# Prompt attention of a hybrid decoder step: a head's weight piece issued behind the AV products instead of right behind the scores

## The reference

```
q, k, v, qi, ki, wi, gq, gk, gv, og, a1, gt = split(h @ w_in)       # one input projection
# branch A: sparse attention; an indexer picks 256 causal keys per query
sc  = where(causal, sum_h wi * relu(qi . ki), -inf);  idx = top_k(sc, 256)
s   = where(valid, q . k[idx] * 64**-0.5, -inf)
att = softmax(s) @ v[idx]                                          # 16 heads, 4 KV heads, head width 64
# branch B: gated linear attention in chunks of 64; gla = rmsnorm(o) * silu(og)
merged = sigmoid(gt0) * (att @ w_proj_attn) + sigmoid(gt1) * (gla @ w_proj_gla)
h = LN(alpha*h + merged @ w_out);  h = LN(alpha*h + relu(h @ w_up)**2 @ w_down)
```

## Time and profile before

| | |
|---|---|
| median of three runs | 3179.45 us (3174.3 to 3191.85) |
| the profiled execution, its own time | 3178.85 us |
| its span in the trace | 3176.9 us |
| mean granted clock of TensorE | 0.924 |
| TensorE matmul busy | 2779.1 us, 87% of the span |
| VectorE, ScalarE, GpSimd busy | 1488.3, 654.4, 569.1 us |
| prompt attention | from about 731 to 1364.8 us |

### The profile page before, as it was taken

How to read it: one execution, slowest core, us unless ns; L and a number is a source line. 1 busy time by engine, 2 the same in 40 slices (tenths; PEclk the granted TensorE clock), 3 DMA queues, 4 the chain that set the end, 5 groups by cost and what they waited for, 6 DMA issues and landing times.

```text
span 3176.9 us, 42244 instructions
## 1 busy us (share of the span) xinstructions
PE 2779.1 (87%) x15803; PEld 2407.3 (76%) x15803; DVE 1488.3 (47%) x2861; ACT 654.4 (21%) x1156; POOL 569.1 (18%) x264
## 2 busy tenths in 40 slices
PE   3968999948999999958889996879899999999996
PEld 3968889948888899845556654769887878788884
DVE  5057999982455545123333425421634343434336
ACT  2033211102233344111223323210310000001011
POOL 4201122210100000100000000122421222222223
PEclk9979999979999999978889968889899999999998
DMA  4142322213211111155434334241111111111001
GB/s 180 56 103 55 105 93 86 85 44 90 76 56 53 31 45 40 55 147 152 143 106 141 113 111 146 99 160 36 39 40 40 40 40 40 40 40 40 26 26 56
DMA packets 173658, 244.03 MB, mean 77 GB/s; under 512 B 49889, under 2 KB 147330, under 8 KB 164146
## 3 DMA queue, kind: packets, MB, share of 16 engines
q1 hardware_dynamic: 139890, 204.03, 20.0%
q10 hardware_dynamic: 33600, 37.80, 3.5%
HBM read 180.00 MB, written 59.08 MB: 75 GB/s over the span
## 4 chain that ended last, share of the span: by engine, by line
PE 65%; DVE 20%; issue 6%; ACT 3%; DMA 2%; SPq 2%; DVEq 2%; POOL 1%; ACTq 0%; POOLq 0%; PEldq 0%
PE ps L955 6%; DVE masks L1694 6%; PE ps L1218 4%; PE ps L1219 4%; PE ps L1220 4%; PE ps L1238 4%; PE ps L1240 3%; PE ps L1239 3%; PE ps L835 2%; DVE maskS L1694 2%; PE ps L836 2%; PE ps L837 2%; PE ps L1059 2%; PE ps L943 2%; PE ps L757 2%
## 5 line engine op out<-in xcount | busy, mean ns | idle before, releaser
L411 POOL TENSOR_TENSOR pool_go<-pool_go 128x1 f32<-128x1 f32 x73 | 15.1, 207 | 2498.0 <-PE ps L837 780.3
L414 POOL TENSOR_TENSOR w_lo<-raw,w_hi 128x2048 fp32r<-128x2048 f32 x73 | 352.8, 4833 | 10.9 <-issue 0.5
L1238 PE MATMUL ps<-w_hi,a_hi 128*128 128x512 f32 (+1 forms) x576 | 241.6, 419 | 66.9 <-DVE res L2080 60.2
L835 PE MATMUL ps<-xt_hi,w_hi 128*128 128x368 f32 x768 | 260.9, 340 | 0.7
L2080 DVE TENSOR_TENSOR res<-res,ps 128x512 f32<-128x512 f32 (+1 forms) x270 | 181.7, 683 | 169.3 <-PE ps L1240 169.3
L1218 PE MATMUL ps<-xt_hi,w_hi 128*128 128x368 f32 x768 | 254.3, 331 | 3.4 <-SPq L368 3.4
L836 PE MATMUL ps<-xt_lo,w_hi 128*128 128x368 f32 x768 | 257.3, 335 | 0.0
L837 PE MATMUL ps<-xt_hi,w_lo 128*128 128x368 f32 x768 | 256.4, 334 | 0.0
L1219 PE MATMUL ps<-xt_lo,w_hi 128*128 128x368 f32 x768 | 254.6, 332 | 0.0
L1220 PE MATMUL ps<-xt_hi,w_lo 128*128 128x368 f32 x768 | 254.1, 331 | 0.0
L1240 PE MATMUL ps<-w_lo,a_hi 128*128 128x512 f32 (+1 forms) x576 | 236.5, 411 | 0.0
(11 more groups left out here) (286 smaller groups left out, 6348.4 us busy)
## 6 DMA issues: line engine op xcount, KB each, us to landing
raw<-w_stream SPq DMA_DIRECT2D x73, 1024.0 KB, 5.0
kpg<-cache_k SPq DMA_DIRECT2D x128, 128.0 KB, 2.2
qT_d<-kT ACTq DMA_DIRECT2D x48, 184.0 KB, 1.9
gate_d<-kT ACTq DMA_DIRECT2D x48, 184.0 KB, 1.9
gst<-gate_d SPq DMA_DIRECT2D x16, 552.0 KB, 5.7
gvog_d<-kT ACTq DMA_DIRECT2D x64, 128.0 KB, 1.9
qraw<-qT_d SPq DMA_DIRECT2D x64, 128.0 KB, 3.1
vpg<-cache_v ACTq DMA_DIRECT2D x64, 128.0 KB, 2.5
```

Source lines behind the costliest of these rows:

```text
L414: pool.tensor_tensor(w_lo[:, s, :], raw[:, s, :], w_hi[:, s, :].bitcast(F32), ALU.subtract).then_inc(w_split, 1)
L835: pe.matmul(out, hi, xt_hi[:, k, cols], start=k == 0, stop=False)
L1238: pe.matmul(out, a_hi[:, a, k, cols], w_hi[:, s, w], start=k == 0, stop=False)
```

## The change

In the loop over head steps on TensorE the piece is issued last, behind the third transpose batch and the AV products of the previous head, instead of right behind the scores. Nothing else is edited.

```diff
@@ -969,13 +969,13 @@
                     tr(hh, j)
                 if hh + 2 < NH * NT:
                     qk(hh + 2)
-                if f < fills_by(hh):
-                    fill(f)
-                    f += 1
                 if nb == 3:
                     tr(hh, 2)
                 for j in range(batches_of((hh - 1) // NH) if hh else 0):
                     av(hh - 1, j)
+                if f < fills_by(hh):
+                    fill(f)
+                    f += 1
             av(NH * NT - 1, 0)
             barrier(pe, 3)
```

## The result

| | before | after |
|---|---|---|
| median of four runs, us | 3176.88 (3172.53 to 3191.85) | 3215.03 (3210.82 to 3236.06) |
| profiled execution, own time | 3178.85 | 3214.59 |
| its span | 3176.9 | 3212.8 |
| mean granted clock | 0.924 | 0.918 |

The ratio is 1.012, 95% interval 1.0079 to 1.0162: slower by 1.2%. The forecast was 3188, with 3176 to 3198 as its range. It had the sign right and the size wrong by a factor of four: the spans differ by 35.9 us where 9 were forecast.

What follows compares the result with a forecast made beforehand. TensorE was taken to bound the loop, waiting mainly for VectorE's query split. Terms 2.5 + 0.2 + 2.5 + 1.2 + 0.4 = 6.8 us, plus 2 for the clock, about 9, gave 3188 us; range 3176 to 3198.

Steps and rivals of the forecast that it cites:

- The swap, 0: Tiles 1 to 7, 28 pieces: swapping AV products and piece on TensorE keeps the sum, 0 us.
- Tile 0, +2.5: Tile 0, heads 1, 5, 9, 13: AV products leave the split's cover, four waits grow by 0.63 us, 2.5 us.
- Tile 8, +0.2: Tile 8: four AV blocks cost 1.0 us, a hidden wait at the end gives -0.81 us; sum +0.2 us.
- GpSimd, +2.5: Three query splits on VectorE collide longer with GpSimd's weight subtraction: +0.85, +1.1, +0.55, sum 2.5 us.
- Exp behind the copy, +1.2: Tile 1, heads 17 to 33: transposes wait for ScalarE's Exp behind its piece copy, 1.2 us.
- Tile 7's last head, +0.4: Third transpose batch, now right behind tile 8's tiny scores, waits for an evacuation, +0.4 us.
- The clock, +2: Longer waits make one or two more stretches at 1.2 GHz likely, 1.25 us lost each: +2 us, ends 0 and 14.
- the difference lies in 731 to 1365 us: The prompt attention loop: a difference outside this stretch would make the whole prediction wrong.
- 26 us is the most the loop could win: Score matmul L927's waits for query split L1766, 26.0 us in 32 times, cap the change's gain, 0.8% of the span.
- B: Rival: eleven grown or new waits each bring a stretch at 1.2 GHz, 14 plus 6.8 us, 3200 us; chance 0.12.
- A: Rival: nothing measurable, moved blocks absorbed because waits end on something that doesn't move with the piece; 3179 us; chance 0.20.
- C: Rival: faster, earlier AV products let VectorE's split go ahead, at most 14 us won, 3165 us; chance 0.04.

Runs made afterwards that it cites:

- e1_tile0: Changed order in tile 0 of the loop alone, otherwise the kernel before: 3177.24 us, loop 626.0 us.
- e3_tile8: Changed order in tile 8 of the loop alone, otherwise the kernel before: 3183.49 us, loop 631.9 us.
- e6_three_back: The kernel after with the pieces of head steps 23, 47 and 71 put back ahead of the AV products: 3217.25 us, loop 651.2 us.
- v1: The kernel before with pieces between transposes and scores in steps hh % 4 == 2, those of tiles 1 to 7 due one step earlier: 3140.44 us, ratio 0.9884.
- e5: The kernel after with ten extra transposes (1.1 us) ahead of the gated linear attention: 3237.51 us, ratio 1.0172.
- e8: The kernel after with 21 extra transposes ahead of gated linear attention head 0 and 26 ahead of each of heads 1 to 3: 3212.74 us, ratio 1.013.
- e2: Changed order in tiles 1 to 7 of the loop alone, otherwise the kernel before: 3210.81 us, loop 642.8 us.
- e11: The kernel after with ten extra transposes (1.1 us) ahead of the head loop: 3216.91 us, loop 649.4 us.
- e7_before_aligned: The kernel before with 26 extra transposes (2.8 us) ahead of each of gated linear attention heads 1, 2 and 3: 3160.29 us, ratio 0.9952.

## Why the prediction was wrong, point by point

1. **The swap, 0.** Nearly. Tiles 5 and 6, with neither half clock nor a changed wait to speak of, grew by 0.24 and 0.28 us with four pieces each: about 0.07 us per piece, 2 us over the 28. It lies inside the bounds of 0.1 us each way; which seam costs it I haven't separated.
2. **Tile 0, +2.5.** Right: 2.07 us per wait where 1.97 was worked out, 28.9 - 26.0 = 2.9 us in e1_tile0. The length didn't show it, since the clock gave as much back (8 us less at 1.2 GHz).
3. **Tile 8, +0.2.** The score waits grew by 1.2 us (e3_tile8; +1.0 was the term). The end went as forecast, with the AV products directly behind the last piece and no wait:

```profile
1379.09 0.33 PE L837 MATMUL ps<-xt_hi,w_lo 128*128 128x368 f32 x1
1379.35 0.35 PE L955 MATMUL ps<-vnat,kT 16*80 16x64 f32 x2
```

   Not foreseen: where the loop's steps are this short the next piece meets the copy of the last one, L835 for L1329, 0.7 us in three times.
4. **GpSimd, +2.5.** The sum was right to a tenth, its parts (0.85, 1.1, 0.55) to 0.16, in both directions; the 1.5 us of the third leaves out the 0.1 us of lead-in and would be 1.6. Timeline of after, tiles 1, 3 and 4:

```profile
844.15 4.50 POOL L414 TENSOR_TENSOR w_lo<-raw,w_hi 128x2048 fp32r<-128x2048 f32 x1
...
845.46 3.75 DVE L1766 TENSOR_TENSOR ql<-qraw,qh 128x512 fp32r<-128x512 f32 x1
...
928.52 2.39 DVE L1766 TENSOR_TENSOR ql<-qraw,qh 128x512 fp32r<-128x512 f32 x1
...
1027.56 1.34 DVE L1766 TENSOR_TENSOR ql<-qraw,qh 128x512 fp32r<-128x512 f32 x1
```

   Against 3.06, 1.23 and 0.68 us that is +0.69, +1.16 and +0.66, 2.5 us. The first ends at 849.21, 0.56 us behind L414's 848.65; the two collisions of before ended 0.56 and 0.54 us behind theirs (847.08 and 925.15); the other two of after end 0.54 us behind theirs (930.37 and 1028.36), though the three of after had started 3.2, 1.9 and 0.8 us ahead of that end. e6_three_back takes exactly these 2.5 us away again. The Trainium skill's page "SBUF — State Buffer" states under "Who interferes with whom" that the later of two such operations is locked out until the other is done, and the sum rested on it; these five collisions with one and the same distance of 0.54 to 0.56 us agree.
5. **Exp behind the copy, +1.2.** The waits at L943 for ScalarE rose by 0.6 us (1.1 after, 0.5 before), of which 0.2 lie at the loop's first transposes, ahead of any piece of it; three of 0.08 us in tile 1 are too short for that row. Half the term.
6. **Tile 7's last head, +0.4.** Right, 0.32 us:

```profile
1282.26 0.33 PE L943 MATMUL ps<-ident,pP 128*128 128x128 f32 x1 [0.32 <-DVE kT L1793]
```

   With these, part 1 and the copies, the direct costs come to 6.6 + 0.6 + 0.7 + 0.3 (less the 0.5 of the earlier trace rows that went, plus 2.0 of the swap), 9.7 us against the 6.8 forecast. Counted the other way, TensorE's idle time in the loop rose from 25.5 to 33.6 us, 8.0, and with the 2.0 of the swap that is 10.
7. **The clock, +2: the term that was mis-sized.** Measured were 18.1 - 9.7 = 8.4 us in the loop, for 19 us more at 1.2 GHz, 0.44 each; 18 starts against 29 had given 0.38. So the price was near, and the amount was not that of one or two stretches of 3.3 us but of about six. It came as two longer stretches in tiles 1 and 3 (10.2 and 13.7 us) rather than as many short ones. I had argued from tile 8's clock of 0.98 that waits of this kind mostly don't bring it on; that row held in one order of the work and not in the other.

**The step that failed altogether** was not in the list: that the difference lies in 731 to 1365 us. The text itself said that the whole would be wrong otherwise. The stages behind were taken to start later and else run as they were, and 22.4 of the 35.9 us came from the one scan that didn't. Without it the spans would differ by 13.5 us, and the time, about 3192, would lie in the range. It could have been priced. The trace of before holds four scans of the same instructions, one of which takes 49.7 us where three take 29.9; I passed over it, because the change doesn't touch that stage. What the runs showed in its place: the scan of head 0 takes 49.8 us after and 29.9 before, by where the granted clock stands when it starts. A range with such a slow scan in it would have reached to about 3188 + 22 = 3210, and with the clock's end of 14 us in the loop beyond 3215.

One more sentence of the prediction fell: that 26 us is the most the loop could win. v1 won 42.7 us there, since each wait costs more than its idle time and brings half clock with it.

**The rivals.** B had the mechanism and too low a price: half clock was 8 us in the loop as it worked out for six stretches, and another 20 us in a place that it didn't name. The Trainium skill's page "TensorE: Matmul & The Clock Gate", section "HAM oscillation — how this bites in real kernels", by which repeated waits bring the half clock back each time, tells of a case with waits of 3 to 5 us each. Here waits of 0.5 to 3.8 us brought it, some of them and not each time: it fits v1 (no wait in the loop, 5 us at 1.2 GHz) and not e1_tile0 (2.9 us more wait, 8 us less at 1.2 GHz). Its "Part 1: The HAM clock gate (the "warmup" mystery)" puts the loss of warming up at under 1% of a typical span and calls it variable from run to run, by the phase in which the kernel starts. Half clock here is not one such loss at the start: this one scan alone turned 0.7% of the span. A fell (waits moved by what was worked out), C fell (no wait shrank).

**What stays open.** Whether a given execution's scan falls to 1.2 GHz: the distance from the last fall sorts the scans afterwards, and nothing here told e5 or e8 ahead. Why the wait ahead of head 0 brings no fall in four of the six traces with late pieces in tiles 1 to 7 (after, e2, e5, e8), and its scan is slow, isn't shown either; e6_three_back, with a loop 7 us longer than after's, escaped. Why the new order has 48 to 72 us of it and the old one 29 to 31 isn't settled either; longer waits are one candidate, yet e6_three_back has shorter waits than after and 20 us more. Each kernel was profiled once, and of the spread from 48 to 72 all but e11's part is that of single executions of one loop program. And the 5 us that the stages behind gave back go with 14 us less at 1.2 GHz there; what moved these stretches isn't known.

## What to carry to other kernels

Price a moved block by what was under its cover, which worked here to 0.1 or 0.2 us per wait, and then look at every stage behind it for equal work that runs at two speeds: there the point at which it starts can be worth more than the edit. Before such a kernel's small gain or loss is put down to an edit, run the kernel before with a delay of its own as a control, and several times, since a single run can't be told from its own spread. And put a filler block on top of the wait, between the last work that is ready and the first that isn't, not on the near or far side of it.

## What the hardware showed that was not expected

- The same scan takes 29.9 or about 49.7 us, by its distance from the last fall of the granted clock: 35 of 36 fast at 8.4 to 9.2 us, 14 of 14 slow at 9.3 to 9.8 us, 6 of 6 slow with no such fall. In the slow case TensorE is busy 98% by the records (50.17 of 51.10 us) and stays at 1.2 GHz for 51.2 us, in all 20 slow scans.
- 8.4 us of added work won 15 to 18 us (e7_before_aligned, eight runs of ten).
- A wait of 0.1 to 0.3 us on TensorE cost about 0.25 us more than its idle time (tiles 5 and 6, before against v1).
- A two-input VectorE operation on a 128x512 tile took 0.68, 1.23, 1.34, 2.39, 3.06 or 3.75 us, by how much of GpSimd's 4.5 us it had to sit out.
